# A hybrid encoder layer on one core: function table loaded ahead, finer first waits, weight sums made by VectorE, bank reads moved ahead

## The reference, cut to what matters

```python
def trunk_layer(x, pos, ...):        # 512 prompt tokens and 8 x 16 sample tokens, D_MODEL 1024, D_FF 2816, float32
    x = x + 0.5 * swiglu(rmsnorm(x, ffn1_norm), ffn1_w_gate, ffn1_w_up, ffn1_w_down)
    h = rmsnorm(x, mix_norm)
    z = h @ w_in                     # gated convolution heads, attention heads, token indexer
    ...                              # convolution, top-256 sparse attention, softmax
    x = x + jnp.concatenate([conv_out, attn], axis=-1) @ w_out
    x = x + 0.5 * swiglu(rmsnorm(x, ffn2_norm), ffn2_w_gate, ffn2_w_up, ffn2_w_down)
    return x, k, v, ki, conv_state

def swiglu(x, w_gate, w_up, w_down):
    return (jax.nn.silu(x @ w_gate) * (x @ w_up)) @ w_down
```

## Time and profile before

| | before |
|---|---|
| median of three runs | 1195.38 us (1193.12 to 1195.83) |
| the profiled execution, its own time | 1193.54 us |
| its span, first to last instruction | 1191.8 us |
| TensorE busy | 1164.2 us, 7800 matmuls |
| VectorE busy | 918.1 us |
| ScalarE busy | 520.4 us |
| GpSimd busy | 280.9 us |
| mean granted clock of TensorE | 0.999 of full |

### The profile page before, as it was taken

How to read it: one execution, slowest core, us unless ns; L and a number is a source line. 1 busy time by engine, 2 the same in 40 slices (tenths; PEclk the granted TensorE clock), 3 DMA queues, 4 the chain that set the end, 5 groups by cost and what they waited for, 6 DMA issues and landing times.

```text
span 1191.8 us, 20543 instructions
## 1 busy us (share of the span) xinstructions
PE 1164.2 (98%) x7800; PEld 1118.0 (94%) x7800; DVE 918.1 (77%) x1261; ACT 520.4 (44%) x787; POOL 280.9 (24%) x217
## 2 busy tenths in 40 slices
PE   8999999999999999999999999999999999999998
PEld 8988999999999999857999689999999999999998
DVE  5898777776989983368998854789877777698995
ACT  5354444444535553351222552534444444444442
POOL 0144454542000000003472000013445444200000
PEclk9999999999999999999999999999999999999999
DMA  7202223222333124211321022321122222224331
GB/s 255 71 36 75 102 70 106 70 80 78 103 147 105 71 88 135 71 36 37 142 72 37 1 65 81 138 84 36 71 106 70 93 83 72 86 98 151 106 94 67
DMA packets 21775, 103.97 MB, mean 87 GB/s; under 512 B 3280, under 2 KB 4688, under 8 KB 12240
## 3 DMA queue, kind: packets, MB, share of 16 engines
q1 hardware_dynamic: 20832, 99.28, 24.1%
q10 hardware_dynamic: 880, 3.82, 1.0%
HBM read 96.99 MB, written 6.10 MB: 87 GB/s over the span
## 4 chain that ended last, share of the span: by engine, by line
PE 85%; DVE 9%; issue 3%; ACT 2%; DMA 1%; ACTq 0%; DVEq 0%
PE ps L583 16%; PE ps L585 16%; PE ps L584 16%; PE ps L545 8%; PE ps L549 8%; PE ps L547 8%; PE ps L536 2%; PE ps L538 2%; PE ps L537 2%; PE ps L778 1%; PE ps L901 1%; DVE wl L1561 1%; PE ps L861 1%; PE ps L787 1%; ACT wh L1021 1%
## 5 line engine op out<-in xcount | busy, mean ns | idle before, releaser
L1021 ACT ACTIVATE wh<-raw 128x1024 fp32r<-128x1024 f32 (+3 forms) x201 | 201.9, 1004 | 282.8 <-PE ps L585 166.1
L583 PE MATMUL ps<-xs,wh 128*128 128x320 f32 x976 | 302.2, 310 | 4.7 <-DVE wl L1561 3.9
L585 PE MATMUL ps<-xs,wl 128*128 128x320 f32 x976 | 301.9, 309 | 0.0
L584 PE MATMUL ps<-xs,wh 128*128 128x320 f32 x976 | 301.8, 309 | 0.0
L583 PEld LDWEIGHTS ps<-xs,wh 128*128 128x128 f32 x976 | 183.6, 188 | 5.8 <-DVE wl L1561 4.7
L585 PEld LDWEIGHTS ps<-xs,wl 128*128 128x128 f32 x976 | 183.6, 188 | 0.0
L584 PEld LDWEIGHTS ps<-xs,wh 128*128 128x128 f32 x976 | 183.5, 188 | 0.0
L1561 DVE TENSOR_TENSOR wl<-raw,wh 128x1024 fp32r<-128x1024 f32 (+1 forms) x108 | 149.3, 1382 | 9.4 <-ACT wh L1021 8.5
L545 PE MATMUL ps<-xh,wh 128*128 128x320 f32 x576 | 137.0, 319 | 2.9 <-DVE wl L1503 2.4
L549 PE MATMUL ps<-xh,wl 128*128 128x320 f32 x576 | 131.2, 309 | 0.0
L547 PE MATMUL ps<-xl,wh 128*128 128x320 f32 x576 | 131.1, 309 | 0.0
(11 more groups left out here) (258 smaller groups left out, 2318.8 us busy)
## 6 DMA issues: line engine op xcount, KB each, us to landing
raw<-gu SPq DMA_DIRECT2D x43, 1024.0 KB, 4.8
raw<-dn SPq DMA_DIRECT2D x16, 1024.0 KB, 4.9
raw<-dn SPq DMA_DIRECT2D x12, 512.0 KB, 3.8
raw<-wconv SPq DMA_DIRECT2D x6, 1024.0 KB, 4.8
raw<-wout SPq DMA_DIRECT2D x4, 1024.0 KB, 5.0
raw<-wtok SPq DMA_DIRECT2D x4, 840.0 KB, 4.3
x<-xt SPq DMA_DIRECT2D x8, 320.0 KB, 4.7
x_keep<-x SPq DMA_DIRECT2D x8, 320.0 KB, 2.2
```

Source lines behind the costliest of these rows:

```text
L583: pe.matmul(out, ah, bh, start=first, stop=False, skip_group_check=True)
L584: pe.matmul(out, ah, bl, start=False, stop=False, skip_group_check=True)
L585: return pe.matmul(out, al, bh, start=False, stop=last, skip_group_check=True)
L1021: return nc.scalar.activation(out, in_, ACT.Copy, scale=scale)
```

## The change

Head: ScalarE waits for the ones tile and applies Tanh to one column, which loads the function table, ahead of its first wait for data. VectorE makes the first weight part's remainder ahead of the first chunk's. TensorE takes chunks 0 to 3 of the first part with a wait for each kind of operand of its own (`first_part_of`).

Sets: GpSimd's `weight_sums` and `set_sums` go. VectorE makes the same four sums (`set_sums`, `set_last_sum`): three at the start of its period for the next set, the last after piece A's remainder. In the first pair the orders differ (`early`, `second`), and the last `plain_hid(3)` moves from the first period to the end of the second.

Down sets: `add_bank(q, 1)` moves ahead of `hid_operand_lo(2, 4)` in set 0, ahead of `hid_operand_lo(2, 2)` in set 3, and in set 4 ahead of piece A of the next set and its last sum; the token sum of set 2 moves behind piece B.

Store: the second half of the last chunk of y is stored ahead of the last wait, the first half after it.

```diff
@@ -522,11 +522,14 @@
             sp.dma_start(ik_out, zki[:, :, 0:HD]).then_inc(kv_stored, 16)
             sp.dma_start(conv_out, cstate[:, :, :, :]).then_inc(kv_stored, 16)
             ffn(1, gu2, dn2, x_keep)
-            for c in range(C):
+            for c in range(C - 1):
                 wait_chunk(sp, 1, c)
                 sp.dma_start(y_out[:, c, :], x[:, c, :]).then_inc(y_stored, 16)
+            sp.dma_start(y_out[:, C - 1, HALF:TOK], x[:, C - 1, HALF:TOK]).then_inc(y_stored, 16)
+            wait_chunk(sp, 1, C - 1)
+            sp.dma_start(y_out[:, C - 1, 0:HALF], x[:, C - 1, 0:HALF]).then_inc(y_stored, 16)
             sp.wait_ge(kv_stored, 64)
-            sp.wait_ge(y_stored, 16 * C)
+            sp.wait_ge(y_stored, 16 * (C + 1))
 
 
         @block.tensor
@@ -571,6 +574,21 @@
                 b = 4 * slot + 2 * m
                 return token_halves((b, b + 1), weight(wh, slot, 8 * m + c), weight(wl, slot, 8 * m + c),
                                     xh[:, c, :], xl[:, c, :], c == 0, c == C - 1)
+
+            def first_part_of(c):
+
+                ah, al, outs = weight(wh, 0, c), weight(wl, 0, c), [ps[:, b, 0:HALF] for b in range(2)]
+                cols = [slice(0, HALF), slice(HALF, TOK)]
+                pe.wait_ge(part_hi, 1)
+                pe.wait_ge(xh_ready, c + 1)
+                for o, t in zip(outs, cols):
+                    pe.matmul(o, ah, xh[:, c, t], start=(c == 0), stop=False)
+                pe.wait_ge(part_lo, 1)
+                for o, t in zip(outs, cols):
+                    pe.matmul(o, al, xh[:, c, t], start=False, stop=False)
+                pe.wait_ge(xl_ready, c + 1)
+                for o, t in zip(outs, cols):
+                    pe.matmul(o, ah, xl[:, c, t], start=False, stop=False)
 
             def glu_unit(slot):
                 for m in range(2):
@@ -694,12 +712,15 @@
                 if k:
                     pe.wait_ge(lo_ready, base + 1)
                 for part, (cs, m) in enumerate((cs, m) for cs in (range(0, 4), range(4, 8)) for m in range(2)):
-                    if k == 0:
+                    if k == 0 and part:
                         pe.wait_ge(*((part_lo, part + 1) if part < 3 else (lo_ready, 1)))
                     if k and cs[0] == 0:
 
                         pe.wait_ge(proj_evac, NPROJ + 2 * NOUT - 1 + m)
                     for c in cs:
+                        if k == 0 and m == 0 and c < 4:
+                            first_part_of(c)
+                            continue
                         if m == 0:
                             pe.wait_ge(xh_ready, C * stage + c + 1)
                             pe.wait_ge(xl_ready, C * stage + c + 1)
@@ -1354,6 +1375,8 @@
             load_x(act, 0)
             act.dma_start(sm[:, :], small).then_inc(small_in, 16)
             load_x(act, 1)
+            act.wait_ge(ones_set, 3)
+            nc.scalar.activation(rstd[:, 0:1], ones[:, 0:1], ACT.Tanh, scale=0.5)
             ffn(0)
 
             for c in range(6, C):
@@ -1496,13 +1519,16 @@
                 base = U_FFN2 * k
                 if k == 0:
                     for c in range(C):
-                        operand_lo(0, c)
+                        if c:
+                            operand_lo(0, c)
                         if c in (0, 1, 4, 5):
                             i = (0, 1, None, None, 2, 3)[c]
                             dve.wait_ge(*((part_hi, i + 1) if i < 3 else (hi_ready, 1)))
                             dve.tensor_tensor(first_part(wl, i), first_part(raw, i),
                                               first_part(wh, i).bitcast(F32), ALU.subtract)\
                                 .then_inc(part_lo if i < 3 else lo_ready, 1)
+                        if c == 0:
+                            operand_lo(0, c)
                     for c in range(1, 4):
                         add_squares(0, c)
                     split_lo(2, 1, 2048)
@@ -1561,6 +1587,26 @@
                     dve.tensor_tensor(ring(wl_flat, part), set_source(slot, part),
                                       ring(wh_flat, part).bitcast(F32), ALU.subtract)\
                         .then_inc(lo_ready if part == 3 else set_lo, 1)
+
+                def set_sums(p, slot):
+
+                    g, h = ALL_SETS * k + 2 * p + slot, base // 2 + PLAIN // 2 + p
+                    a = [raw[:, slot, Q4 * n:Q4 * (n + 1)] for n in range(4)]
+                    s2, s1 = sums[:, 0:Q4], sums[:, Q4:2 * Q4]
+                    dve.wait_ge(raw_in[slot], 16 * (h + slot))
+                    if not (isinstance(g, int) and g == 0):
+                        dve.wait_ge(set_lo, 3 * g - 1)
+                    dve.tensor_tensor(s1, a[2], a[3], ALU.add).then_inc(sum_ready, 1)
+                    dve.tensor_tensor(a[2], a[0], a[2], ALU.subtract).then_inc(sum_ready, 1)
+                    dve.wait_ge(sum_ready, 4 * g + 1)
+                    dve.tensor_tensor(s2, s1, a[0], ALU.subtract).then_inc(sum_ready, 1)
+
+                def set_last_sum(p, slot):
+
+                    g, a = ALL_SETS * k + 2 * p + slot, raw[:, slot, Q4:2 * Q4]
+                    dve.wait_ge(set_lo, 3 * g + 1)
+                    dve.wait_ge(sum_ready, 4 * g + 3)
+                    dve.tensor_tensor(a, a, sums[:, 0:Q4], ALU.subtract).then_inc(sum_ready, 1)
 
                 def hid_at(block, i):
                     return hid[:, bass.ds(block * TOK + (0, TOK + HALF, HALF, TOK)[i], HALF)]
@@ -1594,30 +1640,41 @@
                         dve.tensor_tensor(h, fourth if i == 3 else quart[:, i, :], h, ALU.mult)\
                             .then_inc(pair_hid, 1)
 
-                def period(p, slot, block, ahead=True, early=False):
+                def period(p, slot, block, ahead=True, early=False, second=False):
 
                     np_, ns = (p, 1) if slot == 0 else (p + 1, 0)
+                    if ahead and not early:
+                        set_sums(np_, ns)
                     out_of(p, slot, 0, block)
                     if early:
                         out_of(p, slot, 1, block)
                     if ahead:
                         set_rest(np_, ns, 0)
+                    if early:
+                        set_sums(np_, ns)
+                    if ahead:
+                        set_last_sum(np_, ns)
                     else:
                         rest_lo(0)
                         split_lo(base + GU + 1, 0, 1024)
                     gate_or_mul(p, slot, 0, block)
+                    if early:
+                        out_of(p, slot, 2, block)
+                    if second:
+                        out_of(p, slot, 1, block)
                     if ahead:
                         set_rest(np_, ns, 1)
+                    if not early and not second:
+                        out_of(p, slot, 1, block)
                     if not early:
-                        out_of(p, slot, 1, block)
-                    out_of(p, slot, 2, block)
+                        out_of(p, slot, 2, block)
                     gate_or_mul(p, slot, 1, block)
                     if ahead:
                         set_rest(np_, ns, 2)
-                    if early:
-                        plain_hid(3)
                     gate_or_mul(p, slot, 2, block)
                     gate_or_mul(p, slot, 3, block)
+                    if second:
+                        plain_hid(3)
                     if ahead:
                         set_rest(np_, ns, 3)
                     else:
@@ -1704,34 +1761,36 @@
                     add_bank(q, 0)
                     if q == 4:
                         hid_operand_lo(2, 5)
+                        hid_operand_lo(2, 6)
                     if q == 0:
                         hid_operand_lo(2, 0)
-                    if ahead:
+                    if ahead and q != 4:
+                        down_set_lo(q + 1, 0)
+                        down_last_sum(q + 1)
+                    if q == 1:
+                        dve.wait_ge(xt_ready, 12 * k + 10)
+                        dve.wait_ge(xo_lo, operand_no(k, 2, 0))
+                        token_sum(H_SOURCE[2][2], hid_quadrant(2, 1, 1), H_SOURCE[2][3])
+                    if q == 3:
+                        hid_operand_lo(2, 1)
+                    add_snap(q, 2)
+                    add_snap(q, 1)
+                    add_bank(q, 1)
+                    if q == 4:
                         down_set_lo(q + 1, 0)
                         down_last_sum(q + 1)
                     if q == 0:
                         hid_operand_lo(2, 4)
-                    if q == 1:
-                        dve.wait_ge(xt_ready, 12 * k + 10)
-                        dve.wait_ge(xo_lo, operand_no(k, 2, 0))
-                        token_sum(H_SOURCE[2][2], hid_quadrant(2, 1, 1), H_SOURCE[2][3])
+                    if q == 3:
+                        hid_operand_lo(2, 2)
+                    if ahead:
+                        down_set_lo(q + 1, 1)
+                    elif k == 0:
```

(22 more changed lines are left out.)

19 lines of the change are left out of this document (removed).

## The result

The changed kernel takes **1183.05 us** (median of 5 runs, 1181.73 to 1183.32) against 1195.38 for the kernel before (5 runs, 1193.12 to 1196.04): a ratio of **0.9901**, with a 95% interval from 0.9887 to 0.9914, so 12.3 us faster. The profiled execution took 1183.32 us with a span of 1181.5, 10.3 us less than the span of before.

What follows compares the result with a forecast made beforehand. TensorE, busy 98% of the span, bounds the kernel, so only its waits count. Gains 0 + 5.3 + 3.1 + 5.0 + 0.4 = 13.8 us, taken from the median 1195.38, give 1181.6 us; range 1177.5 to 1187.

Steps and rivals of the forecast that it cites:

- Contention and the sums' price: VectorE beside GpSimd: each GpSimd sum beside VectorE's work costs VectorE 0.98 us; making a sum itself costs 0.68 us.
- rival (c): Steady sets, bank read before the seventh product: VectorE becomes the bound, time about 1195 to 1207 us; chance 0.05.
- First pair: First stage's first two sets: waits on VectorE go, a snapshot wait of 1.3 + 0.28 stays; gain 5.3 us.
- Second pair: Second stage's first two sets: piece D's wait and the clock's fall go, 0.4 + 0.28 stays; gain 3.1 us.
- Down sets: Down sets 0, 3 and 4, both stages: waits go at 0 and 3, 0.70 stays at 4; gain 5.0 us.
- Store: Last store of y: halving what is stored after the last wait; gain 0.4 us, bounds 0 and 0.5.
- Head: Start of the kernel: TensorE starts earlier but waits longer for the sum of squares; gain 0, bounds 0 and 1.5 us.
- Rival (b): Clock falls behind a wait that is left, the head named as risk: once 1183.3 us, twice 1185; chance 0.10.
- The prediction's own sign of being wrong: Any TensorE wait in steady sets, squares ending before 26.8 us, or the clock column below 1 where it was 1.

Runs made afterwards that it cites:

- the kernel with the sums alone: The changed kernel with VectorE's old order in the first two sets of a stage, sums still on VectorE: 1186.35 us, ratio 0.9937.
- the edit of two numbers: The changed kernel with TensorE's sums of squares in the head put two chunks later: 1180.28 us, ratio 0.9889; run again, 1180.98 us.
- the kernel with the order alone: The changed kernel with its four gate and up sums a set given back to GpSimd: 1184.59 us, ratio 0.9928.

## Why the prediction was right, and where not

The forecast was 1181.6 us, in a range from 1177.5 to 1187; measured were 1183.05. Step by step:

- **Contention and the sums' price.** The mechanism is right, now by experiment: 684 ns without GpSimd's sums, 1601 on average with them. Both its sizes were a little off, each in the change's favour. A stretch costs 1.10 us, not 0.98: in a steady set of the kernel before the remainder at 198.99 us takes 1.78 and the gate product behind it 1.59, against 0.68 and 0.48. And a sum costs VectorE 0.60 us, not 0.68, since the three in a row start at 198.82, 199.42 and 200.02 in the changed kernel. So VectorE in the steady sets came to 167.25 / 210 x 12.30 = 9.8 us a set against 10.2 predicted. The margin of rival (c) was never used.
- **First pair.** Forecast 5.3, measured 5.27. The wait that was left, ScalarE's snapshot at 1.3 + 0.28, came as 1.33 + 0.28. It fits better than its working deserves: the sum counted from the order only the 1.7 us of gate product. The bank read that lets ScalarE's third tanh go 0.8 us sooner was missing from it, and the kernel with the sums alone shows that it was needed: without it the wait is 2.28. That the sum hit to 0.03 us is in part luck.
- **Second pair.** Forecast 3.1, measured 2.98; the wait left was 0.51 + 0.28 instead of 0.4 + 0.28. The fall of the clock at 842 went with the wait, as assumed; but the kernel with the head alone kept that wait and had no fall there, so the 1.7 us of it are not in every execution.
- **Down sets.** Forecast 5.0; set 4 waits 0.47 where 0.42 was worked out. Alone it brought 5.5 us in the medians, from which the noise of the clock can't be kept out.
- **Store.** Forecast 0.4. The rest behind the second pair gained 2.97, of which the down sets make 2.5. The DMA view of the changed kernel gives the halves 2.0 us to landing where 320 KB took 2.2. It was not run by itself.
- **Head.** Here a step failed. "None of this reaches the end. Gain 0" was right for the work and left out what the longer wait does: it costs the clock. That step should have read 0 - 1.5. The wait for the squares ended at 27.12 and was 1.23 us, not some 2. The table load came off the path and ScalarE's first copy went at 6.24 instead of 6.75, TensorE's first matmul at 7.64, and 0.29 us were lost to a later landing of x.
- **The clock.** The sum let the fall at 842 go and let no new one come. Rival (b) named the risk, with its place in a sentence of its own, and had a chance of 0.10. It is what happened, twice: about 1.5 us at 29.4 and 1.6 at 657.4. The prediction's own sign of being wrong, a clock column below 1 where it was 1, came true at both. Take both and the 0.29 from the 13.8 and 10.4 us are left; the profiled pair shows 1193.54 - 1183.32 = 10.2.

So the waits were right and the clock was not. The 13.8 us are 12.1 of waits, store included, and 1.7 for the fall at 842. Without any fall the 12.1 hold: the kernel before took 1192.76 us in its two executions at a clock of 1.000, the changed kernel without its head part 1180.20 in its one, 12.6 less, on another chip. At a clock of 0.999 the changed kernel is 11.8 us faster.

That the median came within 1.5 us of the forecast is in part luck. The sum was read from the profiled execution but taken from the median, 1.84 us above it. Taken from the profiled execution it gives 1179.7, and the changed kernel's took 1183.32. The 12.3 us of the medians are those 10.2 plus the 1.84, plus 0.27 by which the changed kernel's profile lies above its median.

## What to carry to other kernels

When a part is made earlier ahead of a wait that doesn't move, TensorE only waits longer, and a longer pause can cost more than itself through the clock: put other matmuls into the pause first, as the edit of two numbers did here, and only then does the earlier start pay. An engine that helps out may cost the helped one more than the work is worth (here 1.10 us for each meeting, against 0.60 for making a sum itself): compare the same instruction with and without company, one by one and not only by the mean, before dividing work between GpSimd and VectorE. And when a wait is named after something that was done over a microsecond earlier, look down the other engines for what ended just before the matmul; then ask whether its whole chain is late, for then moving the one instruction only moves the wait.

## What the runs showed of the hardware that was not expected

- The same wait doesn't always have the same effect on the clock. Behind 1.22 to 1.23 us at 27 us it fell in five of six profiles. Behind 1.8 us of wait at piece D of the second stage it fell in the kernels before and with the new down sets, but not in the one with the new head alone.
- Beside GpSimd's sums a VectorE remainder of 128x512 took either 0.68 us or 1.77 to 1.79, nothing between, in the 36 of the kernel with the order alone; GpSimd's own sums there took 1.39 to 1.73 us on average.
